# Experts with 120 token slots in place of 128 in a mixture-of-experts layer on one core

## The reference, cut to what matters

```python
logits = (ht @ w_router + b_router).astype(jnp.float32)
top_vals, top_idx = lax.top_k(logits, TOP_K)            # TOP_K = 4 of N_EXPERTS = 32
gates = jax.nn.softmax(top_vals, axis=-1)
...
def expert_block(args):
    xblk, e = args                                      # rows of tokens of expert e
    gu = xblk @ w_gate_up[e] + b_gate_up[e]             # [rows, 1024] @ [1024, 2048]
    gate = jnp.minimum(gu[:, :D_EXPERT], SWIGLU_LIMIT)
    up = jnp.clip(gu[:, D_EXPERT:], -SWIGLU_LIMIT, SWIGLU_LIMIT)
    act = gate * jax.nn.sigmoid(SWIGLU_ALPHA * gate) * (up + 1)
    return act @ w_down[e] + b_down[e]                  # [rows, 1024] @ [1024, 1024]
```

## Time and profile before

| | |
|---|---|
| median of 3 runs | 1845.29 us (1844.57 to 1845.68) |
| profiled execution, from first to last instruction | 1846.6 us |
| mean granted TensorE clock | 0.978 of full speed |
| expert turns in the loop (355.42 to 1318.41 us) | 27 of 35.67 us |

### The profile page before, as it was taken

One profiled execution on the slowest core, in us unless ns is written; L12 is line 12 of the kernel. 1 busy time (PEld: TensorE's weight loads), 2 busy tenths in 40 slices (PEclk: granted clock), 3 DMA queues, 4 the chain that ended last, 5 costly groups with the idle time before them and its releaser, 6 DMA issues. The chain is left out here.

```text
span 1846.6 us, 24783 instructions
## 1 busy us (share of the span) xinstructions
PE 1773.2 (96%) x8429; PEld 1393.5 (75%) x8430; DVE 1517.8 (82%) x1693; ACT 1148.1 (62%) x1251; POOL 238.3 (13%) x203
## 2 busy tenths in 40 slices
PE   6988979999999999999999999999999899998998
PEld 3556457888888888888888888888887368887996
DVE  5366657999999999999999999999998647887663
ACT  5343326777777777777777777777774644436541
POOL 0140210000010010000001001000125200004420
PEclk9997969999999999999999999999999899999999
DMA  6032739999999999999999999999997622211001
GB/s 211 11 110 100 310 115 351 395 391 378 388 383 380 383 387 376 378 388 380 381 383 392 370 386 387 376 379 387 391 365 267 203 87 69 92 46 70 1 24 46
DMA packets 104311, 503.94 MB, mean 273 GB/s; under 512 B 18865, under 2 KB 36510, under 8 KB 53986
## 3 DMA queue, kind: packets, MB, share of 16 engines
q1 hardware_dynamic: 97202, 477.56, 67.5%
q0 software_dynamic: 7056, 25.69, 3.9%
HBM read 480.66 MB, written 22.55 MB: 273 GB/s over the span
## 5 line engine op out<-in xcount | busy, mean ns | idle before, releaser
L1761 DVE TENSOR_TENSOR part<-ring,part 128x2048 fp32r<-128x2048 f32 x258 | 584.5, 2287 | 35.4 <-ACT part L1461 35.4
L1461 ACT ACTIVATE part<-ring 128x2048 fp32r<-128x2048 f32 x256 | 486.0, 1919 | 135.1 <-PE bank L1614 75.4
L1591 PE MATMUL bank<-part,xT_hi 128*128 128x512 f32 x1536 | 393.8, 398 | 0.0
L1591 PEld LDWEIGHTS bank<-part,xT_hi 128*128 128x128 f32 x1536 | 284.7, 189 | 59.4
L1461 ACT ACTIVATE part<-rest 128x2048 fp32r<-128x2048 f32 x124 | 238.1, 1922 | 107.7 <-PE bank L1591 81.9
L1761 DVE TENSOR_TENSOR part<-rest,part 128x2048 fp32r<-128x2048 f32 x124 | 281.2, 2291 | 0.0
L1625 PE MATMUL bank<-part,actT_hi 128*128 128x512 f32 x1024 | 276.9, 392 | 0.7 <-DVE part L1761 0.5
L1625 PEld LDWEIGHTS bank<-part,actT_hi 128*128 128x128 f32 x1024 | 189.8, 188 | 39.0 <-issue 0.9
L1918 POOL DMA_INDIRECT rest<-h_rows,rest x33 | 82.6, 2504 | 1031.9 <-PE bank L1574 1016.7
L1591 PE MATMUL bank<-part,xT_lo 128*128 128x512 f32 x768 | 206.5, 391 | 0.0
L1591 PEld LDWEIGHTS bank<-part,xT_lo 128*128 128x128 f32 x768 | 144.7, 188 | 31.0
(11 more groups left out here) (500 smaller groups left out, 2510.4 us busy)
## 6 DMA issues: line engine op xcount, KB each, us to landing
ring<-in_w_gate_up SPq DMA_DIRECT2D x194, 1024.0 KB, 7.9
ring<-in_w_down SPq DMA_DIRECT2D x66, 1024.0 KB, 6.6
rest<-in_w_gate_up SPq DMA_DIRECT2D x62, 1024.0 KB, 8.4
rest<-in_w_down SPq DMA_DIRECT2D x62, 1024.0 KB, 7.1
expert_rows<-rest SPq DMA_DIRECT2D x31, 512.0 KB, 8.5
ring<-in_w_in SPq DMA_DIRECT2D x14, 1024.0 KB, 5.3
rest<-in_w_ada SPq DMA_DIRECT2D x8, 1536.0 KB, 7.4
ring<-in_w_out SPq DMA_DIRECT2D x16, 512.0 KB, 6.4
```

What stands on the lines that cost most here:

```text
L1461: nc.scalar.activation(hi[part(i, c)], raw(i, c), ACT.Copy).then_inc(sig("hi_ready"), counts)
L1591: ins = nc.tensor.matmul(bank[g][:], rows[:, c, :], w[:, g * 512:(g + 1) * 512], start=first, stop=last, skip_group_check=True)
L1761: V.tensor_tensor(lo[part(i, c)], raw(i, c), hi[part(i, c)].bitcast(F32), ALU.subtract).then_inc(sig("lo_ready"), counts)
```

## The change

A constant `CAP = 120` takes the place of 128 as the number of slots of an expert's first block. In the matmuls of a turn the stationary operand has 120 columns and the output 120 partitions; the moving operand stays 512 wide. ScalarE and VectorE work on 120 partitions. The transposes of the activated rows have 120 input partitions and 120 moving columns. The gather, the transposes of the gathered rows, the stores of `y` and all weight loads from memory keep their size. Partitions 96 to 127 of `y` are cleared once by GpSimd, and `copy_y` waits for that. An expert with more than 120 rows now has an extra block, which begins at place 120; counting the blocks takes one instruction more.

```diff
+CAP = 120
...
-            chain.link(V.tensor_scalar(extra, count, float(P), None, ALU.is_gt))
-            chain.link(V.scalar_tensor_tensor(out=extra, in0=count, scalar=2.0 * P, in1=extra, op0=ALU.is_gt, op1=ALU.add))
-            chain.link(V.scalar_tensor_tensor(out=extra, in0=count, scalar=3.0 * P, in1=extra, op0=ALU.is_gt, op1=ALU.add))
+            chain.link(V.tensor_scalar(extra, count, float(CAP), None, ALU.is_gt))
+            chain.link(V.scalar_tensor_tensor(out=extra, in0=count, scalar=float(CAP + P), in1=extra, op0=ALU.is_gt, op1=ALU.add))
+            chain.link(V.scalar_tensor_tensor(out=extra, in0=count, scalar=float(CAP + 2 * P), in1=extra, op0=ALU.is_gt, op1=ALU.add))
+            chain.link(V.scalar_tensor_tensor(out=extra, in0=count, scalar=float(CAP + 3 * P), in1=extra, op0=ALU.is_gt, op1=ALU.add))
...
-    chain.link(V.tensor_scalar(kept, slot, float(P - 1), None, ALU.is_le))
+    chain.link(V.tensor_scalar(kept, slot, float(CAP - 1), None, ALU.is_le))
...
-    chain.link(P_.tensor_scalar(m["extra"][:, 0:MAX_EXTRA], bj, 1.0, float(P), ALU.add, ALU.mult))
+    chain.link(P_.tensor_scalar(m["extra"][:, 0:MAX_EXTRA], bj, float(P), float(CAP), ALU.mult, ALU.add))
...
             chain.link(nc.gpsimd.memset(m["half"], -0.5))
+            nc.gpsimd.memset(y[96:P, :], 0.0).then_inc(sig("y_cleared"), 1)
...
-                    nc.scalar.activation(sigm[:, h, :], bank[h][:], ACT.Sigmoid, scale=ALPHA).then_inc(sig(f"sigm_ready{h}"), 1)
+                    nc.scalar.activation(sigm[0:CAP, h, :], bank[h][0:CAP], ACT.Sigmoid, scale=ALPHA).then_inc(sig(f"sigm_ready{h}"), 1)
...
+                act.wait_ge(sig("y_cleared"), 1)
-                nc.scalar.activation(y[:, 0:512], bank[6][:], ACT.Copy)
+                nc.scalar.activation(y[0:CAP, 0:512], bank[6][0:CAP], ACT.Copy)
...
-                    ins = nc.tensor.transpose(bank[4 + h][:, k * P:(k + 1) * P], cols[:, k // 2, k % 2, :], ident)
+                    ins = nc.tensor.transpose(bank[4 + h][:, k * P:k * P + CAP], cols[:, k // 2, k % 2, :], ident[0:CAP, 0:CAP])
...
-                        ins = nc.tensor.matmul(bank[g][:], rows[:, c, :], w[:, g * 512:(g + 1) * 512], start=first, stop=last, skip_group_check=True)
+                        ins = nc.tensor.matmul(bank[g][0:CAP], rows[:, c, 0:CAP], w[:, g * 512:(g + 1) * 512], start=first, stop=last, skip_group_check=True)
...
-                    nc.tensor.matmul(bank[g][:], pick[0:96, bass.ds(i, 1)].broadcast_to([96, P]), b_gu[0:96, g * 512:(g + 1) * 512], start=False, stop=False, skip_group_check=True)
+                    nc.tensor.matmul(bank[g][0:CAP], pick[0:96, bass.ds(i, 1)].broadcast_to([96, CAP]), b_gu[0:96, g * 512:(g + 1) * 512], start=False, stop=False, skip_group_check=True)
```

More of the change, by code:

```diff
@@ L1482, in copy_y @@
                 act.wait_ge(sig("y_stored"), 16 * i)
-                nc.scalar.activation(y[:, 0:512], bank[6][:], ACT.Copy)
-                nc.scalar.activation(y[:, 512:D], bank[7][:], ACT.Copy).then_inc(sig("y_ready"), 1)
+                act.wait_ge(sig("y_cleared"), 1)
+                nc.scalar.activation(y[0:CAP, 0:512], bank[6][0:CAP], ACT.Copy)
+                nc.scalar.activation(y[0:CAP, 512:D], bank[7][0:CAP], ACT.Copy).then_inc(sig("y_ready"), 1)
             def turn(i):
@@ L1579, in turn_act @@
                 pe.wait_ge(sig(f"act_ready{h}"), n)
-                cols = act_[:, h, :].rearrange("p (c r q) -> p c q r", c=2, q=2)
+                cols = act_[0:CAP, h, :].rearrange("p (c r q) -> p c q r", c=2, q=2)
                 for k in range(4):
-                    ins = nc.tensor.transpose(bank[4 + h][:, k * P:(k + 1) * P], cols[:, k // 2, k % 2, :], ident)
+                    ins = nc.tensor.transpose(bank[4 + h][:, k * P:k * P + CAP], cols[:, k // 2, k % 2, :], ident[0:CAP, 0:CAP])
                 ins.then_inc(sig(f"act_turned{h}"), 1)
@@ L1607, in first_gate_ups @@
                             for g in banks:
-                                nc.tensor.matmul(bank[g][:], xT_hi[:, c, :], w[:, g * 512:(g + 1) * 512], start=(c == 0 and w is w_hi[0]), stop=False, skip_group_check=True)
+                                nc.tensor.matmul(bank[g][0:CAP], xT_hi[:, c, 0:CAP], w[:, g * 512:(g + 1) * 512], start=(c == 0 and w is w_hi[0]), stop=False, skip_group_check=True)
                     if banks == (2, 3):
@@ L1613, in first_gate_ups @@
                         for g in banks:
-                            ins = nc.tensor.matmul(bank[g][:], xT_lo[:, c, :], w_hi[c][:, g * 512:(g + 1) * 512], start=False, stop=False, skip_group_check=True)
+                            ins = nc.tensor.matmul(bank[g][0:CAP], xT_lo[:, c, 0:CAP], w_hi[c][:, g * 512:(g + 1) * 512], start=False, stop=False, skip_group_check=True)
                 ins.then_inc(sig("chunk_used"), 2)
@@ L1624, in down @@
                         for g in range(2):
-                            ins = nc.tensor.matmul(bank[6 + g][:], rows[:, n, :], w[:, k, g * 512:(g + 1) * 512], start=first, stop=last, skip_group_check=True)
+                            ins = nc.tensor.matmul(bank[6 + g][0:CAP], rows[:, n, 0:CAP], w[:, k, g * 512:(g + 1) * 512], start=first, stop=last, skip_group_check=True)
                 ins.then_inc(sig("chunk_used"), counts)
@@ L1776, in clip @@
                 for h in range(2):
-                    V.tensor_scalar(up[:, h, :], bank[2 + h][:], LIMIT + 1.0, 1.0 - LIMIT, ALU.min, ALU.max).then_inc(sig(f"clipped{h}"), 1)
+                    V.tensor_scalar(up[0:CAP, h, :], bank[2 + h][0:CAP], LIMIT + 1.0, 1.0 - LIMIT, ALU.min, ALU.max).then_inc(sig(f"clipped{h}"), 1)
             def gated(i):
@@ L1783, in gated @@
                     dve.wait_ge(sig(f"sigm_ready{h}"), i + 1)
-                    V.scalar_tensor_tensor(out=up[:, h, :], in0=sigm[:, h, :], scalar=SIGM_MAX, in1=up[:, h, :], op0=ALU.min, op1=ALU.mult).then_inc(sig(f"gated{h}"), 1)
+                    V.scalar_tensor_tensor(out=up[0:CAP, h, :], in0=sigm[0:CAP, h, :], scalar=SIGM_MAX, in1=up[0:CAP, h, :], op0=ALU.min, op1=ALU.mult).then_inc(sig(f"gated{h}"), 1)
             def times_gate(i):
@@ L1789, in times_gate @@
                     dve.wait_ge(sig(f"gated{h}"), i + 1)
-                    V.scalar_tensor_tensor(out=act_[:, h, :], in0=bank[h][:], scalar=LIMIT, in1=up[:, h, :], op0=ALU.min, op1=ALU.mult).then_inc(sig(f"act_ready{h}"), 1)
+                    V.scalar_tensor_tensor(out=act_[0:CAP, h, :], in0=bank[h][0:CAP], scalar=LIMIT, in1=up[0:CAP, h, :], op0=ALU.min, op1=ALU.mult).then_inc(sig(f"act_ready{h}"), 1)
             def rows_lo(n):
```

## The result

The changed kernel takes 1872.66 us (median of 4 runs, 1871.04 to 1872.76) against 1845.49 us before (4 runs): a ratio of 1.0144, 95% interval 1.0132 to 1.0156, 27 us slower. The forecast was 1845.8 us and no measurable change; the time lies above the range too (1826 to 1856).

A forecast was written before the change was run, and what follows sets the result against it. PE's instruction stream, never idle in a turn, was taken to bound the kernel. Weight load -2.4, bias loads +2.7 and slowed list instructions +0.2 gave +0.5 us on 1845.3: 1845.8 us, range 1826 to 1856.

The forecast's parts named there:

- the first term: Expert matmuls: a weight load 6.4 ns shorter brings each of 4608 matmuls 0.53 ns nearer, -2.4 us.
- the 13.4 ns over the stream: Expert matmuls: distance of 226.7 ns less 213.3 ns for streaming 512 columns; some of it might hang on the weight load.
- The slower-rhythm rival: Expert matmuls: loads of another length bring the 231 ns distance seen at L695, 4.3 ns more, +20 us, 1865 us; chance 0.11.
- The full-load rival: Expert matmuls: the shorter load shows whole in the distance, -29.5 us, 1816 us; chance 0.26 for any share above 0.8 ns.
- The plain matmuls: Float32 matmuls that aren't split: 434 ns apart at 64 and 32 columns, 427 at 128, taken as evidence that columns cost nothing.
- The bias term: Four bias matmuls a turn: loads go from 98 to 182 ns, the first uncovered on PE's stream, 32 x 84 ns, +2.7 us.
- The small terms: Transposes, ScalarE and VectorE on 120 partitions, GpSimd's fill, the extra count, DMA: together +0.2 us, all of it from the fill.
- The fill: GpSimd's clearing of `y`, 32 x 1024, before the gather: 1.0 us, hidden in the gather's wait of 4.01 us for PE's transposes.
- VectorE's four list instructions: Start of the expert phase: 0.87 us, PE waits for them; slowed by GpSimd's fill by 0 to 0.4 us, taken as 0.2.
- The extra count: One more counting instruction on VectorE: 0.20 us, hidden in the 3.40 us that VectorE waits for PE.
- the transposes: Eight a turn of the activated rows, moving side 128 to 120: taken as nothing, in proportion 2.2 us less.
- No extra block: Fullest expert holds 116 rows, so none expected at 120; with other inputs 1878 us or more, chance 0.02.

The follow-up runs named there:

- e6: Changed kernel, 120 columns kept, with the tiles of the stationary operands moved by 8 words (32 bytes): 1844.87 us, ratio 0.9994 to the kernel before.
- e1: Split matmuls alone, both blocks of the kernel left out, stationary columns varied from 128 to 32: 226.7 ns apart at 128, 233.3 at 120.
- e5: Split matmuls alone, loaded columns or moving rows shifted in memory: 128 columns 226.7 ns unmoved, 233.4 moved 8 words; 120 columns 233.3 and 226.7.
- e2: Changed kernel with its matmuls alone back at 128 stationary columns, all other edits kept: 1847.33 us, ratio 1.0006 to the kernel before.
- e7: Kernel before, 128 columns, with the tiles of the stationary operands moved by 8 words: 1870.64 us, ratio 1.0135 to the kernel before.

## Why the prediction was wrong

What bounds the kernel was right: PE's stream, without idle time, before and after. A nanosecond per matmul was worth about its 4.6 us: 5.5 ns a matmul make 25 us.

The step that failed is the first term, the weight load's share in the distance: -0.53 ns a matmul, -2.4 us, read from a slope between two kinds of matmul, with nothing and -6.4 ns as bounds. That another load could lengthen the distance had no place in this term. The distance measured +6.6 ns within `down`, and 0.79 us / 144 = 5.5 ns over a turn, some +25 us.

The load itself shortened as estimated, 188 to 182 ns. The Trainium skill's page "TensorE: Matmul & The Clock Gate", section "LDWEIGHTS (loading the stationary operand)", has a load take columns / 1.2 ns, an estimated 6.7 ns for 8 columns. The trace agrees with that difference, but not with the whole: 128 columns would take an estimated 107 ns by the rule and take 188 here.

What failed is the idea that the 13.4 ns over the stream are a share of the load's duration. In e6 the load is the shorter one, 182 ns, and the distance is the old 226.7: with each count at a good place the share is nothing. Narrower moving operands show it too, 256 columns in e1 (two lines are 12 matmuls apart, then the loads of the same stretch) and a block of 48 with 384 columns in e5:

```profile
251.02 1.12 PE L263 MATMUL bank<-part,xT_hi 128*128 128x256 f32 x8
...
252.46 1.12 PE L263 MATMUL bank<-part,xT_hi 128*128 128x256 f32 x8
```

```profile
L263 PEld LDWEIGHTS bank<-part,xT_hi 128*128 128x128 f32 x40 | 5.2, 192 | 0.0
```

```profile
637.25 8.57 PE L263 MATMUL bank<-part,xT_hi 128*128 128x384 f32 x48
```

With 256, 384 and 512 moving columns, 128 stationary ones run 1.44 / 12 = 120.0, 173.3 and 226.7 ns apart. Each 128 columns add 53.3 ns, one column per cycle at 2.4 GHz as the prediction supposed, and each time 13.3 ns remain. At 256 the distance is shorter than the 192 ns that the profile gives for a load, so the two durations can't simply be set against each other. With the place of the load and with its count the 13.3 ns grow to as much as 21 (234.3 ns), and in e1 no load has a shorter distance than the longest one.

The slower-rhythm rival came nearest, with too little chance (0.11) and too low a price: 4.3 ns (20 us), taken from the stage of the earlier trace rows, where up to 7.6 ns were possible. What it supposed, that loads of another length bring the rhythm, is not the cause either: 120 columns run at both distances. The range ended at about half of that rival, and so missed. The rows against it (27 equal turns) showed only that a rhythm lasts, not that it survives another load. The full-load rival, -29.5 us, finds no support: e1 has no slope at 512 moving columns. The plain matmuls were indeed deaf to the column count, but they are another kind. By their single starts they are 429 ns apart at 32, 64 and 128 columns; the 434 and 427 are quotients of a group's busy time. Read in the same way, the bias matmuls are 222 ns apart on average and not 219, which would have made the first term -1.6 us in place of -2.4.

The bias term, +2.7 us, was wrong. The load of 120 two-byte columns takes 133 ns, where 98 and 182 were the bounds. The Trainium skill's page "TensorE: Matmul & The Clock Gate", section "Weight-path perf modes — Fast Weight Load (FWL) and DoubleRow", has the fast load only where the number of weights is 128; the trace agrees, with 98 ns at 128 columns. What failed is that the longer load would lie bare on PE's stream: it costs nothing there. PE and weight loads of one turn after the change (answers to the earlier trace rows):

```profile
825.96 1.03 PE L1636 MATMUL bank<-rest 96*120 96x512 bf16 x4
826.64 0.58 PE L1597 MATMUL bank<-part,xT_hi 128*120 128x512 f32 x1
```

```profile
825.73 0.80 PEld L1636 LDWEIGHTS bank<-rest 96*120 x4
```

The first load now begins 0.23 us ahead of its matmul (825.73 to 825.96) where it began 0.01 us ahead before, so it is covered, and the four matmuls take 0.68 us to the next one, 0.69 before. In the other runs the early start goes with the bias load's 120 columns too: 0.22 us in e6, under 0.01 in e2 and e7, where it has 128. Why is not shown.

The small terms held. Where the expert phase begins (answers to the earlier trace rows):

```profile
268.76 0.95 POOL L1414 MEMSET rest<- 32x1024 f32 x1
268.93 1.32 DVE L1772 TENSOR_SCALAR rest<-rest 128x128 f16<-128x128 f32 x4 [2.36 <-PEq L177]
...
273.14 0.96 POOL L1924 DMA_INDIRECT rest<-h_rows,rest  x1 [3.43 <-PE bank L1580]
```

The fill takes 0.95 us (1.0 forecast) inside the gather's wait, which is still 3.43 us; VectorE's four list instructions beside it went from 0.87 to 1.32 us, 0.45 us (0.2 forecast, 0.4 the bound, so just over it). The extra count went into VectorE's wait, and the transposes and the 120 partitions cost nothing that e2 can tell. No extra block came up: there are the same 194 + 62 loads of `w_gate_up`.

What stays open is why 8 words decide. The experiments show that the load's place against the moving rows, modulo 256 bytes, and the column count set the distance together, and that it is the same with all other engines quiet. What in the memory or in the engine makes it so was not seen. The map isn't complete either: 127 columns ran at 226.7 ns in e1 and at 233.3 in e5, 124 at 228.3 and 226.7, where the loads came in another order.

## What to carry to other kernels

When PE has no idle time, the distance between matmuls is the quantity to measure, not the duration of the loads beside them: look for it in the order of time, and see whether it is even. A distance over the bare stream is not a price list of the hidden load. If the stationary tiles change in size or place, try the tile some words further on before giving the change its verdict: here a move of 32 bytes took away 28 us in one kernel and cost 25 us in the other. A slower rhythm seen in a stage with other tiles doesn't bound how slow it can get: 231 ns there, up to 234.3 here.

## What the runs showed of the hardware that was not expected

Float32 split matmuls with 512 moving columns have no single distance at one clock: it was anything from 226.7 to 234.3 ns by place and count, most often 226.7 or 233.4, and never below 226.7 in the kinds tried. With 256 moving columns the count does show, 120.0 ns at 128 columns, 117.3 at 120 and 113.3 at 64 (e1, at one place each). VectorE's list instructions took half as long again beside GpSimd's fill of 0.95 us: 1.32 us in all six whole-kernel traces with the fill, 0.87 us in both without it.
